# Taking out the matmuls of constants that stand in TensorE's waits in a two-layer hybrid backbone

## Chip, core and metric

The kernel runs on one core of a Trainium2 chip. The metric is the device time of one execution in microseconds, here the median of three timed runs. One more execution was recorded by the hardware profiler; its rows are what the argument uses.

## What is computed

Two layers of a trunk over 512 latent tokens with 256 context tokens ahead of them, model width 1024, all in float32. The reference, cut to the frame of a layer:

```
for l in range(DEPTH):                      # DEPTH = 2
    hx = modulate(rms_norm(x, norm_mix_pre[l]), sh1x, sc1x)
    hc = modulate(rms_norm(h_ctx, norm_mix_pre[l]), sh1c, sc1c)
    y_x, y_c = mixing_layer(hx, hc, ...)    # three head groups, one w_in, one w_out
    x = x + g1x * rms_norm(y_x, norm_mix_post[l])
    hx = modulate(rms_norm(x, norm_mlp_pre[l]), sh2x, sc2x)
    x = x + g2x * rms_norm(sq_relu_mlp(hx, w_mlp1[l], w_mlp2[l]), norm_mlp_post[l])
    if want_ctx: ...                        # the same for h_ctx, layer 1 only
...
def mixing_layer(...):
    zx = split_cols(hx @ w_in_l, IN_SIZES)
    gdn  = gdn_mixer(...)    # gated DeltaNet: triangular solves per chunk, then a scan both ways
    mla  = mla_mixer(...)    # latent attention: softmax(q k^T) v, 4 heads
    hgrn = hgrn_mixer(...)   # HGRN2: gated linear recurrence both ways
    return concatenate([gdn, mla, hgrn]) @ w_out_l
```

The shifts, scales and gates (`sh1x` and so on) come from `silu(c) @ w_ada[l]`.

## The kernel before

All five engines run hand-written queues; an engine waits on counters (semaphores) that others raise. Nothing reorders the work: what stands behind a waiting instruction on its engine waits too. The tokens lie along the columns: a product of 128 rows of outputs has 768 columns (256 of the context, 512 latent), written as two matmuls into a pair of PSUM banks. The second layer leaves out the context where it isn't needed.

The large matrices are multiplied as sums of products of a high and a low part (three matmuls per block of 128 inputs, type float32r, one TensorE instruction each). Plain float32 matmuls take two TensorE instructions each; transposes take one.

The order of a layer on TensorE: the sum of squares of the first norm (`norm0`, in `sum_squares`, lines 900 to 914), the input projection (`gemm_entry`, line 859, which goes through the inputs block by block as POOL and DVE deliver them, then `gemm_parts`), the chunk matrices and triangular inverses of the DeltaNet (lines 1045 to 1148; line 1147 works on blocks which ACT, DVE and POOL have spread out before), its scan, the projection and the levels of the HGRN2 (`level_product`, lines 1294 to 1316: a product of small 32x32 or 64x64 blocks, then DVE and ACT make the factors of the next level from the former ones), `turn_keys` (line 1334, transposes), the sum of squares of its output (`hrms`), attention (`scores`, transposes of the probabilities at line 1457, `output`), the output projection, and the MLP (`mlp_start`, line 1509, and the loop at line 1565). `grms` is the sum of squares of the DeltaNet's output. Columns of `w_ada` for the next modulation (line 970) are worked off in between.

The helper that the change concerns is `hold_clock(dst, n)` (line 832). It issues n matmuls of the constant matrix `ones` with a slice of a constants tile into a piece of PSUM that is free there and is overwritten later with `start=True`; nobody reads the result. It raises no counter. It is called at ten places: at the entry of the input projection (4 in layer 1, 6 in layer 2), ahead of the sums of squares `norm0` (0 and 6), `grms` (3) and `hrms` (1), ahead of line 1045 (1), after the 32x32 inverses (2), in the levels (6 in layer 1), in `turn_keys` (3 and 2), in the first attention steps (4 and 3) and in the MLP's first products (0 and 6). The calls stand between two waits: the first, for the PSUM bank, holds for the filling product too; the second, for the operands, only for the real product behind it. That makes 54 matmuls, 108 TensorE instructions.

## Time and profile before

| | us |
|---|---|
| three timed runs, median | 2350.25 |
| lowest and highest of them | 2344.41, 2350.57 |
| profiled execution | 2344.16 |
| its span, first to last instruction | 2342.3 |
| TensorE busy in it | 2236.3 |
| VectorE, ScalarE, GpSimd busy | 1172.5, 860.8, 222.6 |

The profile names engines by their short names: PE is TensorE's matmuls, PEld its weight loads (which overlap), DVE VectorE, ACT ScalarE, POOL GpSimd, SP the queue that issues DMAs. Times in rows are microseconds from the span's start, unless "ns" is said. PEclk is the granted TensorE clock, 1.00 for 2.4 GHz and 0.50 for 1.2 GHz. The end of a matmul is modelled, and matmuls overlap, so the time that one costs is read from the starts of neighbours. "x12" says that a row merges twelve instructions.

### The profile page before, as it was taken

To read this page: it belongs to the slowest core of one execution; us is meant where nothing else is said; L and a number is where in the kernel's file an instruction comes from. 1 tells how busy PE (TensorE), PEld (TensorE's weight loads), DVE (VectorE), ACT (ScalarE), POOL (GpSimd) and SP (SyncE) were. 2 spreads that over 40 slices of the span, in tenths; PEclk is the share of its full clock that TensorE was granted. 3 is DMA by queue.
4 is the path that set the end of the run, shared out by engine and by line. 5 is a ranking of instruction groups with operands and counts; after the bars stand their busy time and mean duration, and the time that the engine had idled before them with its cause. 6 is when DMAs were issued, how large, how long until landed. Compare 5 with 4: busy or idle time off the path is not lost.

```text
span 2342.3 us, 43142 instructions
## 1 busy us (share of the span) xinstructions
PE 2236.3 (95%) x19310; PEld 1818.3 (78%) x19310; DVE 1172.5 (50%) x1848; ACT 860.8 (37%) x1250; POOL 222.6 (10%) x218
## 2 busy tenths in 40 slices
PE   8999899989999999999999999889997999999998
PEld 5876598876668788888888677659785669888887
DVE  4674353188363651424233587536248456444444
ACT  5362134225464421212123546232324456222233
POOL 3013410000030100000000011421000021000000
PEclk9999999999999999999999999999999999999999
DMA  9217101134301121212121221411116301323222
GB/s 320 64 63 269 53 17 55 55 110 141 104 16 37 37 90 55 72 55 72 54 72 55 91 80 37 150 53 36 55 55 213 120 19 55 108 91 107 90 90 72
DMA packets 161694, 198.42 MB, mean 85 GB/s; under 512 B 18358, under 2 KB 129432, under 8 KB 160871
## 3 DMA queue, kind: packets, MB, share of 16 engines
q1 hardware_dynamic: 155536, 185.20, 24.4%
q10 hardware_dynamic: 5271, 10.10, 1.3%
q8 instruction: 152, 2.49, 0.4%
q0 software_dynamic: 704, 0.37, 0.2%
q14 instruction: 31, 0.25, 0.0%
HBM read 184.60 MB, written 11.06 MB: 84 GB/s over the span
## 4 chain that ended last, share of the span: by engine, by line
PE 86%; DVE 6%; ACT 4%; issue 3%; DMA 0%; POOL 0%; DVEq 0%; ACTq 0%
PE ps L1565 35%; PE ps L857 15%; PE ps L1483 5%; PE ps L1098 3%; PE ps L911 2%; PE ps L1522 2%; PE ps L1418 2%; PE ps L970 2%; PE ps L1237 1%; PE ps L844 1%; PE ps L835 1%; DVE region L2533 1%; PE ps L873 1%; PE ps L1431 1%; PE ps L1457 1%
## 5 line engine op out<-in xcount | busy, mean ns | idle before, releaser
L1565 PE MATMUL ps<-region_r 128*128 128x512 f32 (+1 forms) x1536 | 376.7, 354 | 0.0
L1565 PEld LDWEIGHTS ps<-region_r 128*128 128x128 f32 x1536 | 270.3, 188 | 40.7
L1565 PE MATMUL ps<-region_r,weights_r 128*128 128x512 f32 (+1 forms) x768 | 229.6, 353 | 0.0
L2184 DVE TENSOR_TENSOR weights_r<-weights,region_r 128x2048 fp32r<-128x2048 f32 x62 | 141.9, 2289 | 119.9 <-ACT region_r L1701 119.9
L1565 PE MATMUL ps<-mixed_r,weights_r 128*128 128x512 f32 (+1 forms) x672 | 200.9, 354 | 0.0
L1565 PE MATMUL ps<-modulated_r,region_r 128*128 128x256 f32 (+1 forms) x624 | 186.7, 354 | 0.0
L1565 PE MATMUL ps<-mixed_r,region_r 128*128 128x256 f32 (+1 forms) x624 | 186.6, 353 | 0.0
L2112 ACT ACTIVATE region<-ps,cst 128x768 f32<-128x768 f32 (+1 forms) x64 | 50.2, 795 | 300.8 <-PE ps L1565 281.3
L1565 PEld LDWEIGHTS ps<-region_r,weights_r 128*128 128x128 f32 x768 | 144.3, 188 | 20.5
L2692 DVE TENSOR_TENSOR region_r<-region 128x768 fp32r<-128x768 f32 (+1 forms) x64 | 52.8, 824 | 203.0 <-ACT region L2112 203.0
L1565 PEld LDWEIGHTS ps<-mixed_r,weights_r 128*128 128x128 f32 x672 | 126.3, 188 | 18.0
L1565 PEld LDWEIGHTS ps<-mixed_r,region_r 128*128 128x128 f32 x624 | 117.3, 188 | 16.6
L1565 PEld LDWEIGHTS ps<-modulated_r,region_r 128*128 128x128 f32 x624 | 117.3, 188 | 16.6
L1701 ACT ACTIVATE region_r<-weights 128x2048 fp32r<-128x2048 f32 x62 | 118.5, 1910 | 12.8 <-DMA weights<-in_w_mlp 12.8
L857 PE MATMUL ps<-residual_r,weights_r 128*128 128x512 f32 (+1 forms) x432 | 117.4, 344 | 0.0
L2118 ACT ACTIVATE region<-ps 128x768 f32<-128x768 f32 (+1 forms) x48 | 33.8, 705 | 218.2 <-PE ps L1565 218.2
L2699 DVE TENSOR_TENSOR region<-region 128x768 f32<-128x768 f32 (+1 forms) x32 | 26.4, 825 | 138.9 <-ACT region L2118 138.9
L857 PEld LDWEIGHTS ps<-residual_r,weights_r 128*128 128x128 f32 x432 | 81.1, 188 | 10.6 <-issue 0.2
L857 PE MATMUL ps<-region_r,weights_r 128*128 128x256 f32 x320 | 81.7, 337 | 0.0
L725 POOL CAST region_r<-modulated 128x768 fp32r<-128x768 f32 x16 | 22.7, 1461 | 576.6 <-ACT modulated L1743 576.6
L1098 PE MATMUL ps<-modulated,weights 128*128 128x512 f32 x128 | 69.1, 637 | 5.2 <-issue 4.4
L2191 DVE TENSOR_TENSOR weights_r<-weights,state_r 128x2048 fp32r<-128x2048 f32 x14 | 32.1, 2292 | 82.2 <-ACT state_r L1687 82.2
(435 smaller groups left out, 4809.5 us busy)
## 6 DMA issues: line engine op xcount, KB each, us to landing
weights<-in_w_mlp SPq DMA_DIRECT2D x64, 1024.0 KB, 5.6
weights<-in_w_ada SPq DMA_DIRECT2D x40, 1024.0 KB, 6.1
weights<-in_w_in SPq DMA_DIRECT2D x34, 1024.0 KB, 5.4
region<-in_w_ada SPq DMA_DIRECT2D x8, 1024.0 KB, 16.9
weights<-in_w_out SPq DMA_DIRECT2D x8, 1024.0 KB, 6.7
x_kept<-residual SPq DMA_DIRECT2D x2, 3072.0 KB, 12.4
region<-decays_kept ACTq DMA_DIRECT2D x4, 1536.0 KB, 10.6
residual<-x_kept SPq DMA_DIRECT2D x2, 3072.0 KB, 10.5
```

Of the source, the lines that this page charges most:

```text
L857: last = mm(dst[:, CTX + a:CTX + b], w[:, k, m], r[k][:, a:b], start=(k == 0 and w is high and r is r_high), stop=(k == KB - 1 and r is r_ ...
L911: last = mm(dst[:, CTX + a:CTX + b], mat, sq[:, a:b], start=(k == 0), stop=(k == n - 1))
L970: last = mm(ps[32 * k:32 * k + 32, bank, :], cs[:, 4 * half + k, :], w[:, k, :], start=(half == 0), stop=(half == 1))
L1098: last = mm(ps[:, 6, :], w, Hm[:, k, CTX:TOK], start=(k == 0), stop=(k == KB - 1))
L1418: last = mm(dst[:, CTX + s0:CTX + s1], QH[0:96, h, 128 * qt:128 * qt + 128], KH[0:96, h, s0:s1], start=True, stop=True)
L1483: last = mm(dst[:, at:at + b - a], w[:, k, m], r[:, a:b], start=(k == 0 and part_of == "low"), stop=(k == 5 and w is low))
L1522: last = mm(o, w[:, k, m], r[:, k, a:b], start=(k == 0 and r is Hm_r), stop=(k == KB - 1 and w is low))
L1565: last = mm(dst[:, CTX + a:CTX + b], w[:, k, m], r[:, a:b], start=(k == 0 and r is r_low), stop=(k == KB - 1 and w is low))
L1701: af(mlp_high(j), ring[:, n % NSLOT, :], ACT.Copy).then_inc(w_high_ready, 1)
L2112: copied(l, what, u, af(hid[:, b, lo:], src, ACT.Relu, bias=zero_col))
L2184: v.tensor_tensor(ring_r[:, at, :], ring[:, at, :], mlp_high(j), ALU.subtract).then_inc(w_low_ready, 1)
L2692: v.tensor_tensor(hid_high[:, b, lo:], z, z, ALU.mult)
```

## The change

The helper and all its calls go, with the tables that hold their counts. The waits that stood around a call stay, one behind the other. No other engine's code changes, and no other matmul moves against another.

```diff
-            def hold_clock(dst, n):
-
-                for _ in range(n):
-                    mm(dst, ones, kf[:, 4:8, :].rearrange("p a b -> p (a b)")[:, 0:dst.shape[1]], start=True, stop=True)
...
                 dst = [free_pair(l, "qkv", u) for u in units]
-                hold_clock(dst[0][:, 512:1024], 4 + 2 * l)
...
-                if n0 == 0:
-                    hold_clock(dst[:, 512:1024], {"norm0": 6 * l, "grms": 3, "hrms": 1}.get(what, 0))
...
                 pe.wait_ge(gemm_evac, number(UNITS, l, "qkv", 11) - 2)
-                hold_clock(pair(number(UNITS, l, "qkv", 11) + 1)[:, 512:1024], 1)
                 pe.wait_ge(gs_ready, l + 1)
...
                         pe.wait_ge(u_ready, 2 * NS * (l + 1))
-                        hold_clock(ps[:, 0, :], 2)
                         pe.wait_ge(spread, 12 * (l + 1))
...
-                LEVEL_HOLDS, HOLDS_FROM = ((1, 1, 1), (0, 0)), (5, 2)
...
-                    if lv >= HOLDS_FROM[l]:
-                        hold_clock(ps[:, bank, :], LEVEL_HOLDS[l][j])
                     pe.wait_ge(m_ready, item(l, lv, j))
...
-                    if k < 2:
-                        hold_clock(ps[:, k, :], ((1, 2), (2, 0))[l][k])
...
-                FIRST_HOLDS = ((1, 1, 1, 1), (1, 1, 1, 0))
...
-                    hold_clock(dst[:, 512:1024], FIRST_HOLDS[l][i] if i < 4 else 0)
                     pe.wait_ge(p_ready, a + 1)
...
-                    if p == 1:
-                        hold_clock(dst[0], 6 * l)
```

On TensorE, in the last two levels of layer 1, the queue before reads as follows (`region` holds the factors, `weights,silu_c` are columns of `w_ada`):

```order
2103 L970 MATMUL ps<-weights,silu_c 32x512 x4
2104 L835 MATMUL ps<-k_f_sb 128x512
2105 L1309 MATMUL ps<-region 32x32 x32
2106 L835 MATMUL ps<-k_f_sb 128x512
2107 L1309 MATMUL ps<-region 32x32 x32
2108 L970 MATMUL ps<-weights,silu_c 32x512 x4
2109 L835 MATMUL ps<-k_f_sb 128x512
2110 L1309 MATMUL ps<-region 32x32 x32
2111 L977 MATMUL ps<-row_select,state 128x2 x4
2112 L970 MATMUL ps<-weights,silu_c 32x512 x4
2113 L835 MATMUL ps<-k_f_sb 128x512
2114 L1313 MATMUL ps<-region 64x64 x16
```

and with the change (its lines are numbered anew):

```order
2099 L962 MATMUL ps<-weights,silu_c 32x512 x4
2100 L1296 MATMUL ps<-region 32x32 x64
2101 L962 MATMUL ps<-weights,silu_c 32x512 x4
2102 L1296 MATMUL ps<-region 32x32 x32
2103 L969 MATMUL ps<-row_select,state 128x2 x4
2104 L962 MATMUL ps<-weights,silu_c 32x512 x4
2105 L1300 MATMUL ps<-region 64x64 x32
```

The filling products are gone, and the small products stand directly behind those of `w_ada` or behind each other.

## Rows read from the trace of the kernel before

In a timeline a row gives start, length, engine, line, operation, what is written and read, and in brackets the engine's idle time ahead of it with what ended it. A row of stretches gives the stretch, its length, the busy time (and the instructions) of PE, PEld, DVE, ACT and POOL, then PEclk, the share of the DMA engines and GB/s. A row of waits gives total, times, longest.

**Rows 1.** The page: engines' busy time, chain that ended last.

```profile
span 2342.3 us, 43142 instructions
...
PE 2236.3 (95%) x19310; PEld 1818.3 (78%) x19310; DVE 1172.5 (50%) x1848; ACT 860.8 (37%) x1250; POOL 222.6 (10%) x218
...
PE 86%; DVE 6%; ACT 4%; issue 3%; DMA 0%; POOL 0%; DVEq 0%; ACTq 0%
```

**Rows 2.** All products of line 835, one line's view (durations in ns).

```profile
L835 PE MATMUL ps<-k_f_sb x108: 379/592/697, 42.5 to 1985.5; 128*128 128x512 f32 x96, 128*128 128x256 f32 x12
```

**Rows 3.** Timeline 40 to 50 us: start, us, engine line op, [idle before].

```profile
42.52 3.68 PE L835 MATMUL ps<-k_f_sb 128*128 128x512 f32 x8
...
46.41 0.58 PE L873 MATMUL ps<-region_r,state_r 128*128 128x256 f32 x2 [0.22 <-POOL region_r L725]
```

**Rows 4.** Timeline 1320 to 1372 us.

```profile
1325.24 5.31 PE L835 MATMUL ps<-k_f_sb 128*128 128x512 f32 x12
...
1333.49 12.28 PE L911 MATMUL ps<-mixed,k_f_sb 128*128 128x256 f32 x32 [2.94 <-ACT mixed L1774]
...
1346.86 5.39 PE L835 MATMUL ps<-k_f_sb 128*128 128x512 f32 x12 [1.08 <-ACT region L1656]
...
1350.13 0.96 POOL L725 CAST region_r<-modulated 128x768 fp32r<-128x768 f32 x1 [541.84 <-ACT modulated L1743]
...
1351.68 0.80 PE L873 MATMUL ps<-region_r,state_r 128*128 128x512 f32 x1
```

**Rows 5.** Timeline 289 to 293 us.

```profile
289.46 2.00 ACT L1905 ACTIVATE residual<-ps 32x384 f32<-32x384 f32 x4 [0.40 <-PE ps L1135]
...
290.48 1.98 PE L835 MATMUL ps<-k_f_sb 128*128 128x512 f32 x4 [1.22 <-DVE mixed L2417]
...
292.39 0.27 PE L1147 MATMUL ps<-mixed,region 64*64 64x64 f32 x1
```

**Rows 6.** Timeline 585.6 to 588.5 us.

```profile
586.25 1.58 ACT L1628 ACTIVATE region<-mixed 128x768 f32<-128x768 f32 x2 [7.74 <-DVE mixed L2593]
...
586.76 1.13 PE L835 MATMUL ps<-k_f_sb 128*128 128x512 f32 x2 [1.02 <-DVE cst L2600]
```

**Rows 7.** Timeline 640 to 652 us, first attention steps.

```profile
640.37 1.12 PE L835 MATMUL ps<-k_f_sb 128*128 128x512 f32 x2 [0.59 <-ACT region L2040]
...
644.30 1.91 ACT L1693 ACTIVATE region_r<-weights 128x2048 fp32r<-128x2048 f32 x1
```

**Rows 8.** Busy time in stretches, with the granted clock.

```profile
220.50:227.10 6.60, 3.39 (x63) 2.00 (x66) 0.56 (x1) 0.00 (x0) 1.26 (x1) 1.00 0.37 137
...
522.50:529.33 6.83, 6.23 (x173) 4.49 (x176) 5.29 (x12) 1.94 (x4) 0.00 (x0) 0.50 0.61 197
...
1334.88:1338.29 3.41, 3.41 (x7) 2.02 (x6) 3.41 (x5) 1.71 (x3) 0.00 (x0) 0.50 0.00 0
1491.90:1495.30 3.40, 0.00 (x0) 0.00 (x0) 3.32 (x10) 0.00 (x0) 0.00 (x0) 1.00 0.00 0
1495.30:1498.70 3.40, 2.82 (x4) 1.17 (x4) 0.43 (x4) 2.04 (x3) 0.00 (x0) 0.50 0.55 198
798.98:802.39 3.41, 3.41 (x10) 2.63 (x9) 3.41 (x6) 1.68 (x3) 1.38 (x2) 0.50 0.00 0
802.39:805.80 3.41, 3.41 (x17) 2.81 (x16) 3.41 (x5) 1.77 (x3) 1.38 (x2) 1.00 0.00 0
541.70:565.70 24.00, 21.95 (x371) 11.84 (x367) 20.58 (x49) 18.45 (x41) 0.00 (x0) 1.00 0.60 200
```

**Rows 9.** Timeline 1794 to 1806 us, end of the levels.

```profile
1797.97 1.98 PE L835 MATMUL ps<-k_f_sb 128*128 128x512 f32 x4
...
1801.67 0.66 PE L1347 MATMUL ps<-k_f_sb,region 128*128 128x128 f32 x4 [0.41 <-ACT mixed L2009]
```

**Rows 10.** The core's span and mean granted clock.

```profile
core 0: 2342.3 us, clock 0.990
```

**Rows 11.** Who waited for whom, PE, longest in total.

```profile
PE ps L1309 <- issue: 13.2, 8, 3.4
```

## Prediction

> **What bounds the kernel now.** I read the page first: TensorE is busy 95% of the span and the chain of work that ended last is 86% TensorE [rows 1]. So almost all of the time is matmuls that stand in one queue, and a product that nobody reads costs its length unless the engine would have waited there anyway. The view of line 835 comes next: 108 instructions (54 products of constants, two instructions each), from 42.5 us to 1985.5 us [rows 2]. They stand in 28 groups. Twelve of them take 5.3 us, 0.44 us each [rows 4], so all of them hold the engine for some 47 us, 2% of the span. The question is how much of that was a wait in any case. For that I went through the timeline at each of the 28 groups and compared the start of the next real product with the moment at which the thing it waits for was done. Last I read the granted clock in short stretches [rows 8], because without these products the engine stands idle for longer, and in this trace its clock stands at the lower of its two levels (1.2 instead of 2.4 GHz) in some short stretches.
>
> **What the removal gives back, kind by kind.**
> (a) *Groups inside a wait.* At 42.52 us eight instructions end before the next product starts at 46.41, which POOL releases, with 0.22 us of idle time still in front of it [rows 3]. The twelve at 1325.24 end 2.94 us before the product at 1333.49, which waits for an ACT square [rows 4]. Four more groups look like this (two of 2 instructions ahead of line 1045, two of 6 ahead of the sum of squares of `grms`, with 0.4 to 0.9 us still idle), and so does the group of 12 short ones at the last layer's MLP, behind which the next product starts as DVE delivers. That is 48 of the 108 instructions, and they give back nothing: the releaser is another engine that does not wait for them. What covers them is the normalisation chain on ACT, DVE and POOL.
> (b) *The diagonal blocks' copy.* The four instructions at 290.48 run until the next product at 292.39, while the last of ACT's four copies ends at 289.46 + 2.00 = 291.46 [rows 5]. Without them the product starts some 0.9 us earlier; the same place in the second layer gives 1.0. Together 1.9 us.
> (c) *The sum of squares of `hrms`.* The product behind the two instructions at 586.76 needs the first of two ACT squares, done at about 586.25 + 0.8 = 587.1, and starts when they are through, at 587.7 [rows 6]. That is 0.6 us, in both layers 1.2 us.
> (d) *The entry of layer 2.* The twelve at 1346.86 are followed by the product at 1351.68 with no idle time, but the first POOL cast it reads is only ready at 1350.13 + 0.96 = 1351.09 [rows 4]. So 5 us of filling hide a real wait of almost the same length, and 0.5 us comes back.
> (e) *The levels of layer 1.* Eighteen instructions stand between 541.7 and 563.9 us, about 9 us of TensorE's time, all without idle time around them. But this is a ping-pong with DVE, which is busy 20.58 of 24.00 us there [rows 8]. The gain cannot be over DVE's idle 3.4 us. It may be nothing, if the next DVE step is late for another reason. I take 1.2 us, a third of the slack, since ACT too is at 18.45 of 24.00 and is waited for at the end of the stretch. In layer 2 the four at 1797.97 take 1.8 us, but the product at 1801.67 waits for ACT [rows 9], which is in one piece of work since before them: nothing.
> (f) *The first attention steps.* Seven groups of two, 0.9 us each, 6.5 us in sum, again without idle time behind them (the first is at 640.37 [rows 7]). In layer 1 ACT has a weight conversion of 1.91 us from 644.30 on in its queue [rows 7], and the evacuation of the transposes stands behind it, so what the first steps gain is waited for again. Between 0.5 and 6.5 us; I take 3.0 us (1.2 in layer 1, 1.8 in layer 2), nearer the lower end for that reason.
> Sum of the gains: 1.9 + 1.2 + 0.5 + 1.2 + 3.0 = **7.8 us**, with ends at 4 us (1.9 + 1.2 + 0.5 + 0 + 0.5) and 15 us (3.6 + 3.4 + 1.8 + 6.5).
>
> **What the clock takes.** The mean granted clock is 0.990 [rows 10]: 2342 x 0.010 = 23 us lost, so 47 us at half, some 7 of them at the very end, where nothing dense runs. That is about eleven low stretches of 3.41 us now. The price of one low stretch: from 798.98 to 802.39 the clock is at half and 10 products start, in the equally long stretch after it 17 [rows 8]. Seven of 17 lost in 3.41 us is 1.4 us, and half of 3.41 us, 1.7 us, is the most. I take 1.5 us where dense products follow.
> How often? Before, the engine is idle 3.40 us and more ahead of 1495.3 and the clock is low from there on; it is low from 522.50 to 529.33 behind an idle time of 3.4 us (the longest of line 1309 [rows 11]), and from 1334.88 on behind the 2.94 us at 1333.49 [rows 4, 8]. From 220.5 on TensorE stands still for 3.2 of 6.6 us, waiting for its instructions, and the clock stays up [rows 8]. So of four idle times of 2.9 us and more three were followed by a low stretch. After the removal there are: 42.65 to 46.4 (3.7 us) [rows 3] and three like it of 3.0 to 3.4 us (the two ahead of `grms` and the last MLP): 4 x 0.75 = 3.0 low stretches. 1345.77 to 1351.1 (5.3 us) [rows 4]: 1. The 8.1 us ahead of 1333.49 already had one; what follows there waits for an ACT square every 1.7 us, so a longer low stretch costs about a third of one. Four of 1.8 to 2.3 us (ahead of line 1045 and at the place of (b)), a size behind which the clock mostly stayed up: 1.3. The levels and the attention steps, where 9 and 6.5 us of dense products go out between small ones: 1.5. In sum 7.1 low stretches, x 1.5 us = **10.7 us**. Bounds: 2 stretches (3 us) and 14 (21 us).
>
> **Sum.** -7.8 + 10.7 = +2.9 us. The profiled execution took 2344.2 us (span 2342.3), so it would be 2347.1 with the change; it is at the lower edge of the three timed runs, whose median, 2350.25, lies 6.1 us higher, and I add the difference to that median: **2353 us**. A measurement of this kernel can tell about 0.3%, 7 us, from no change, and the forecast lies inside that.
>
> **Rivals.**
> *Slower, by the clock everywhere.* Place: the first dense products behind each wait that was filled. If every one of the 6 long idle times is followed by a low stretch, the 4 middle ones too, and the levels and attention steps of both layers add 4, that is 14 x 1.5 = 21 us against 7.8: +13 us, 2363 us. It decides from (7.05 + 7.8) / 1.5, about 10 low stretches more than now. For it: three of four; the weak filling that is left between waits in the levels; and a low stretch slows the products that others wait for. Against it: 220.5 us, and that a part of a low stretch falls into the idle time itself and costs nothing.
> The Trainium skill, page "TensorE: Matmul & The Clock Gate", section "HAM oscillation — how this bites in real kernels", says that TensorE's clock is halved after a longer wait and that each burst then starts slow, every time. That rule speaks against this change and would make it this rival; the trace agrees in three of the four long idle times and not in the one at 220.5 us.
> *Faster, the clock hardly reacts.* If only one or two new low stretches appear, mostly inside idle time, cost 0 to 2 us, the gains of 7.8 us remain or are somewhat larger: 2343 us or less. Against it: the idle times of 3.7, 5.3 and 8.1 us.
> *The gains do not arrive.* TensorE waits 13.2 us at line 1309 with the releaser "issue" [rows 11], that is, for nothing that the profile shows but its own instructions. If filling products gave that supply time to catch up, the gain of (e) and part of (f) turn into such waits: gains 5 us, +6 us, 2356 us. This stays within 0.3% alone and is in the forecast's chance.
>
> **Chances.** Forecast (within 0.3%, with the third rival in it) 0.52, slower 0.38, faster 0.10. The range reaches from the edge of the faster rival, 2343, to a little above the slower one's value, 2365, since one time in ten may lie beyond either end.
>
> **What would show it.** In the trace after: no line 835, TensorE busy for some 45 to 50 us less by the page's count apart from slower products; idle times of about 3.7 us ahead of the first product of the entry, 8 and 5.3 us around 1325 to 1351, and the waits of (a) with the same releasers. For the gains: the product behind ACT's copies at 291.5, the one of `hrms` 0.6 us earlier. For the price: 15 to 21 low stretches in place of eleven, with half as many products in those that follow the entries of both layers. The prediction is wrong if the number of low stretches grows by over 10 or by less than 2, or if one of them lasts for several times 3.4 us, or if the levels shrink by far over 3.4 us.

## The result and the profile after

The change makes the kernel slower: 2366.29 us against 2347.78 us for the kernel before on the same chip (medians of six runs each), a ratio of 1.0087 with a 95% interval of 1.0073 to 1.0101, that is about 20 us (18.5 us by the medians). The forecast was 2353 us, a step of 2.9 us up (a ratio of 1.0012) that could not be told from no change, with a range up to 2365 us. What came is clear of no change, and the time lies outside the range.

Some words are used throughout. A *filling product* is one of the 54 that `hold_clock` issues. A *low period* is an unbroken time at half clock, and a *stretch* is 3.41 us of it, the shortest that these traces show. A *place* is a part of the kernel, found again in each trace by its products. "Waits without a releaser" are those which the profile marks "issue".

In this section and the next the lines are those of the changed kernel, numbered anew: 867 for 873 (first products of the input projection), 903 for 911 (sums of squares), 1089 for 1098 (the gate's products between the inverses), 1113, 1123 and 1138 for 1122, 1132 and 1148 (inverses), 1296 and 1300 for 1309 and 1313 (levels). First its page, and its clock, to be held against [rows 1, 10]:

```profile
span 2364.7 us, 42940 instructions
...
PE 2221.9 (94%) x19202; PEld 1820.8 (77%) x19202; DVE 1173.0 (50%) x1848; ACT 861.3 (36%) x1250; POOL 222.4 (9%) x218
...
PE 86%; ACT 5%; DVE 4%; issue 3%; DMA 1%; POOL 0%; DVEq 0%; ACTq 0%
```

```profile
core 0: 2364.7 us, clock 0.973
```

TensorE has 108 instructions less and is busy 14.4 us less, not the 45 to 50 us that the filling products held, while the span is 22.4 us longer than 2342.3. The clock fell from 0.990 to 0.973: 0.027 x 2364.7 = 64 us lost against 23 us, so 128 us at half in place of 47. Read period by period, the clock was low in 25 periods, against 11 before. Without the last one of each, in the tail, where nothing dense runs, they come to 117 us against 35.5 us: 24 low stretches of 3.41 us more. Nine of the 24 periods ahead of the tail are longer than one stretch (6.8 or 10.2 us).

Some of the periods, as busy time in windows of the trace (columns as in [rows 8]; the last four columns are POOL's busy time, the clock, the DMA engines' share and GB/s). After:

```profile
45.00:51.85 6.85, 5.09 (x16) 4.44 (x17) 6.06 (x5) 6.85 (x12) 6.85 (x6) 0.50 1.01 430
51.85:58.70 6.85, 6.85 (x41) 6.00 (x41) 6.85 (x6) 3.15 (x4) 4.52 (x4) 1.00 0.06 22
573.00:595.30 22.30, 22.30 (x234) 22.23 (x234) 12.87 (x41) 7.26 (x11) 0.00 (x0) 0.85 0.01 1
1580.50:1598.80 18.30, 15.50 (x247) 13.67 (x243) 5.07 (x12) 10.87 (x21) 2.04 (x2) 0.81 0.08 29
1338.70:1348.90 10.20, 4.37 (x7) 2.53 (x8) 10.20 (x13) 8.84 (x8) 0.00 (x0) 0.50 0.00 1
```

The same products before, in the entry of layer 1, the state updates and outputs of the HGRN2 behind `turn_keys` (called the read-out below) and the end of layer 2's inverses:

```profile
46.40:53.20 6.80, 6.79 (x39) 5.98 (x40) 6.80 (x5) 6.80 (x12) 6.80 (x6) 1.00 0.83 354
566.00:585.00 19.00, 19.00 (x234) 18.93 (x233) 12.87 (x41) 7.11 (x11) 0.00 (x0) 1.00 0.01 2
1563.00:1576.40 13.40, 13.40 (x247) 11.92 (x244) 5.07 (x12) 10.89 (x21) 2.04 (x2) 1.00 0.02 6
```

The pairs are the first two rows of after with the first of before, the third with the second, the fourth with the third; the last row of after is the one at `norm0` of layer 2. The read-out gives the price cleanly. The same 234 products, all without idle time, take 19.00 us at full clock and 22.30 us with 6.8 us at half: 3.30 us for two stretches, 1.65 us each. At the end of the inverses 247 products go from 13.40 us to 18.30 us. Of these 4.9 us, 2.8 us are time in which TensorE is not busy (15.50 of 18.30), and 2.1 us are slower products.

Some of the waits of TensorE in the whole run after (total, times, longest):

```profile
PE ps L1296 <- issue: 16.1, 11, 3.1
PE ps L903 <- ACT region L1609: 10.8, 6, 3.5
PE ps L867 <- POOL region_r L725: 9.2, 2, 5.5
PE ps L903 <- ACT mixed L1755: 8.2, 1, 8.2
```

Of the lower three little was to be seen before: at the same line TensorE waited 2.3 us in sum for ACT's squares, 2.9 us at the one of `norm0` [rows 4], and for POOL 0.22 us at the first entry [rows 3]; the rest of the time was filled. The first row answers to [rows 11], with eleven waits for eight.

Holding the start of each product against that of the same product before gives the 22.4 us by place. "Low" is the change in time at half clock.

| place, in us of before | span, us | low, us | predicted here, us |
|---|---|---|---|
| start and entry of layer 1 (to 58) | +2.6 | +6.8 | +1.1 |
| norm and first inverses of layer 1 (169 to 306), gain (b) | +1.9 | +6.8 | -0.9, +1.1 |
| `grms`, layer 1 (390 to 400) | +1.4 | +3.4 | +1.1 |
| scan and projection (400 to 541), no filling there | +3.5 | +3.9 | 0 |
| levels, layer 1 (541 to 566), gain (e) | -2.5 | +2.9 | -1.2 and a share of +2.2 |
| read-out of the HGRN2 (566 to 585) | +3.3 | +6.8 | |
| `hrms` and attention, layer 1 (585 to 652), gains (c), (f) | 0.0 | +6.8 | -1.8 and a share of +2.2 |
| MLP of layer 1 (652 to 1324), no filling there | +0.7 | 0.0 | 0 |
| `norm0`, layer 2 (1324 to 1345) | +0.5 | +6.8 | +0.5 |
| entry of layer 2 (1345 to 1365), gain (d) | +0.7 | +3.5 | +1.0 |
| inverses of layer 2 (1490 to 1577), gain (b) | +10.3 | +20.4 | -1.0, +0.9 |
| `grms` to the levels, layer 2 (1577 to 1804) | -0.5 | +6.9 | +1.1 |
| read-out, `hrms`, attention, layer 2 (1804 to 1982) | -1.1 | +3.4 | -2.4 |
| MLP entry, layer 2 (1982 to 1995) | +1.5 | +3.4 | +1.1 |

Nearly half of the loss stands in one place, the triangular inverses of layer 2, where only two of the 54 products were taken out. A second profile of each kernel shows what of this repeats: after again has +9.7 us there, and the kernel before once has +3.2 us against itself. Over the span the second profiles are 2357.1 us (clock 0.975) and 2345.8 us (0.989).

### The profile page after: what moved, and what is told of

The parts are those of the page before. It is cut to its first block, busy times and chain, and to the rows that moved or that the text cites. A ratio compares the mean times of both kernels' runs of the same rounds, so it can differ in the third digit from the quotient of the medians.

```text
span 2364.7 us, 42940 instructions
## 1 busy us (share of the span) xinstructions
PE 2221.9 (94%) x19202; PEld 1820.8 (77%) x19202; DVE 1173.0 (50%) x1848; ACT 861.3 (36%) x1250; POOL 222.4 (9%) x218
## 4 chain that ended last, share of the span: by engine, by line
PE 86%; ACT 5%; DVE 4%; issue 3%; DMA 1%; POOL 0%; DVEq 0%; ACTq 0%
PE ps L1546 35%; PE ps L852 15%; PE ps L1466 4%; PE ps L1089 3%; PE ps L903 2%; PE ps L962 2%; PE ps L1503 2%; PE ps L1403 2%; PE ps L1227 1%; PE ps L867 1%; PE ps L1245 1%; PE ps L839 1%; PE ps L1416 1%; PE ps L1440 1%; PE ps L1346 1%
## 5 line engine op out<-in xcount | busy, mean ns | idle before, releaser
L852 PEld LDWEIGHTS ps<-residual_r,weights_r 128*128 128x128 f32 x432 | 81.1, 188 | 10.5 <-issue 0.2
## 6 DMA issues: line engine op xcount, KB each, us to landing
region<-decays_kept ACTq DMA_DIRECT2D x4, 1536.0 KB, 10.7
residual<-x_kept SPq DMA_DIRECT2D x2, 3072.0 KB, 10.2
```

Of the source, the lines that this page charges most:

```text
L852: last = mm(dst[:, CTX + a:CTX + b], w[:, k, m], r[k][:, a:b], start=(k == 0 and w is high and r is r_high), stop=(k == KB - 1 and r is r_ ...
```

## Experiments

None of the experiments changes a result that is used, since nobody reads the filling products. Edits are against the kernel before, and "..." marks what is left out between their parts. The time that stands behind "against" is the median of the kernel before, measured together with the experiment. Figures by place are against the first profile of the kernel before.

### Which group of products matters

**e1_long** keeps the 28 products in the long waits (entries, `norm0`, `grms`, MLP) and takes the other 26 out:

```diff
-                    hold_clock(dst[:, 512:1024], {"norm0": 6 * l, "grms": 3, "hrms": 1}.get(what, 0))
+                    hold_clock(dst[:, 512:1024], {"norm0": 6 * l, "grms": 3, "hrms": 0}.get(what, 0))
...
-                hold_clock(pair(number(UNITS, l, "qkv", 11) + 1)[:, 512:1024], 1)
...
-                        hold_clock(ps[:, 0, :], 2)
...
-                LEVEL_HOLDS, HOLDS_FROM = ((1, 1, 1), (0, 0)), (5, 2)
+                LEVEL_HOLDS, HOLDS_FROM = ((0, 0, 0), (0, 0)), (5, 2)
...
-                        hold_clock(ps[:, k, :], ((1, 2), (2, 0))[l][k])
+                        hold_clock(ps[:, k, :], ((0, 0), (0, 0))[l][k])
...
-                FIRST_HOLDS = ((1, 1, 1, 1), (1, 1, 1, 0))
+                FIRST_HOLDS = ((0, 0, 0, 0), (0, 0, 0, 0))
```

> Of the 54 filling products of before, 28 are kept, those in the long waits: entry of the input projection, norm0, grms, the MLP's first products. The rest is out, as in the changed kernel. Local theory (each filling keeps the clock up only for the products right behind its own wait): in the comparison of the two traces the stretches behind these waits cost +2.3 us (to 57.6), +1.4 (390 to 399), +0.7 (1334 to 1365) and +1.5 us (1982 to 1995), and up to 1.7 us between 400 and 500; these 6 to 8 us come back, so 2359 us, with 26 or so low stretches of 3.41 us. Rival (low stretches come by where the run happens to stand against the chip's own time, and move whenever a kernel changes): the low stretches of 1501 to 1577 move or go as well, the sum is anywhere between 2350 and 2366, and the stages named don't answer one by one.

Measured: 2356.62 us against 2346.84, ratio 1.0054 [1.0030, 1.0078], clock 0.983. Entries, `grms`, and the MLP entry are back at 0.0 us; the read-out has +3.3 us as after, the inverses of layer 2 +6.7 us. So the fillings of the long waits account for a part, and more than a half of the loss comes with them in place.

**e2_steps** keeps only the 18 products of the levels, `turn_keys` and attention:

```diff
-                hold_clock(dst[0][:, 512:1024], 4 + 2 * l)
...
-                    hold_clock(dst[:, 512:1024], {"norm0": 6 * l, "grms": 3, "hrms": 1}.get(what, 0))
+                    hold_clock(dst[:, 512:1024], {"norm0": 0, "grms": 0, "hrms": 0}.get(what, 0))
...
-                hold_clock(pair(number(UNITS, l, "qkv", 11) + 1)[:, 512:1024], 1)
...
-                        hold_clock(ps[:, 0, :], 2)
...
-                        hold_clock(dst[0], 6 * l)
+                        pass
```

> Kept are the 18 filling products of the levels, turn_keys and the first attention steps; the 36 others are out. Local theory: the stage from 541 to 652 us, which came out at about +0.8 us in sum with gains of 2.5 and 0.9 us and losses of 3.3 and 1.3 us, goes back to before's; in layer 2 the attention's gain of 1.6 us is given up. About 2366 us, as the changed kernel within 2 us. Rival: as for e1_long, low stretches elsewhere move by chance, 2355 to 2370.

Measured: 2366.37 us, 1.0095 [1.0072, 1.0118], clock 0.971. The total came as expected, by way of two misses that the expectation did not have: the read-out has +4.9 us although its fillings stand as before, and the inverses of layer 2 +7.8 us.

**e3_gdn** keeps only the eight products of the DeltaNet's inverses and `hrms` (in each layer one ahead of line 1045, two ahead of line 1147 and one in `hrms`):

```diff
-                hold_clock(dst[0][:, 512:1024], 4 + 2 * l)
...
-                    hold_clock(dst[:, 512:1024], {"norm0": 6 * l, "grms": 3, "hrms": 1}.get(what, 0))
+                    hold_clock(dst[:, 512:1024], {"norm0": 0, "grms": 0, "hrms": 1}.get(what, 0))
...
-                LEVEL_HOLDS, HOLDS_FROM = ((1, 1, 1), (0, 0)), (5, 2)
+                LEVEL_HOLDS, HOLDS_FROM = ((0, 0, 0), (0, 0)), (5, 2)
...
-                        hold_clock(ps[:, k, :], ((1, 2), (2, 0))[l][k])
+                        hold_clock(ps[:, k, :], ((0, 0), (0, 0))[l][k])
...
-                FIRST_HOLDS = ((1, 1, 1, 1), (1, 1, 1, 0))
+                FIRST_HOLDS = ((0, 0, 0, 0), (0, 0, 0, 0))
...
-                        hold_clock(dst[0], 6 * l)
+                        pass
```

> Kept are the 8 filling products ahead of line 1045, ahead of line 1147 (after the inverses) and ahead of the hrms sum; the 46 others are out. Local theory: the stages 289 to 306 and 1559 to 1577 go from +0.2 and +4.0 us to zero, so some 4 us come back, 2362 us; the +6.5 us between 1490 and 1550, where no filling stood in either kernel, stay. Rival: the stages from 1490 to 1577 change together, since what matters is where the low stretches begin, and 6 to 10 us come back or none.

Measured: 2369.95 us, 1.0111 [1.0092, 1.0129], clock 0.971. Expected was 2362: a clear miss. The end of the inverses, with its two filling products in front as before, is longer by 4.8 us. Its window, to be held against the last row of before above, except that it also takes in three of the four filling instructions:

```profile
1582.60:1600.80 18.20, 16.87 (x250) 13.37 (x250) 5.07 (x12) 10.90 (x22) 2.04 (x2) 0.85 0.04 12
```

The timeline says where the 4.8 us lie: 2.9 us between the first filling instruction and the second, of which 2.75 us are a wait without a releaser that ends at 1583.93, 1.3 us in the three filling instructions behind it, which run at half clock, and only 0.6 us behind the filling.

**e4_no_inv2** takes out only these two products, in layer 2:

```diff
-                        hold_clock(ps[:, 0, :], 2)
+                        hold_clock(ps[:, 0, :], 2 * (1 - l))
```

> The kernel before, without the two filling products ahead of line 1147 in layer 2 alone (4 of 108 instructions). Local theory: the stretch 1563 to 1577 loses 5.0 us and the wait gives back 1.0: +4 us, 2352 us, with one more low stretch of 6.8 us and nothing else changed. Rival (the 5.0 us of the changed kernel came of where the low stretches stood after 18 us of delay, not of the two products): within 1 us of before.

Measured: 2349.43 us, 1.0011 [1.0000, 1.0022]; the end of the inverses +0.8 us, the whole place +1.0 us. The local theory, by which each filled wait keeps the clock up for the stage behind it, expected 4 us here. Its step from the missing filling to a low period is borne out: a stretch is low from 1568.2 us, right behind the place of the two products, and costs 1.8 us against the 0.9 us gained. In all six profiles without the two (this one, both of after, e1, e2, e5) a low period lies there, with them in two of ten (e3, e11). The size is what falls: the 5 us that after loses there are not reached without the others, and keeping the two in e3 does not save the place. In after and in e3 a wait without a releaser of 2.8 us stands there, which e4 does not have.

### The place in the instruction stream

If it is not the filling in front alone, it may be something that shifts with the number of filling products. Each of them is four instructions of TensorE's stream (two weight loads, two matmuls), and the inverses are 32x32 and 64x64 products that go out in bursts, between which TensorE waits for nothing that the profile shows. These waits in the inverses of layer 2, before and after:

```profile
PE ps L1122 <- issue: 5.0, 5, 1.3
PE ps L1098 <- issue: 4.4, 1, 4.4
PE ps L1132 <- issue: 3.0, 5, 1.0
```

```profile
PE ps L1113 <- issue: 6.0, 4, 2.9
PE ps L1089 <- issue: 4.4, 1, 4.4
PE ps L1123 <- issue: 3.7, 4, 1.6
PE ps L1138 <- issue: 2.8, 1, 2.8
```

The 4.4 us at line 1098 (1089 after) are in both, and are a wait for DVE, as e11_placed shows below; they are left out of what is called the waits without a releaser of this stage. The rest is 8.0 us before, 12.5 us after (8.1 and 13.9 us in the second profiles); that of after includes the 2.8 us at line 1138 that ate gain (b) there.

**e5_same_count** puts in the place of each product the same number of instructions, waits on a counter that has long been high enough (two such waits share one instruction):

```diff
-                for _ in range(n):
-                    mm(dst, ones, kf[:, 4:8, :].rearrange("p a b -> p (a b)")[:, 0:dst.shape[1]], start=True, stop=True)
+                for _ in range(8 * n):
+                    pe.wait_ge(const_in, 16)
```

> The changed kernel's matmuls, with every filling product replaced by as many TensorE instructions that only wait for a counter which was reached long ago. So the instruction stream has the length and the places of before, and nothing fills. Stream theory: part of the 19 us is not the clock but TensorE's own instruction supply (waits with the releaser issue grew from 7.5 to 12.2 us between 1500 and 1584), which hangs on where in the stream the bursts of small products stand; then those waits go back to about 7 us there, the stage loses its 9.6 us in large part, and the time is 2354 to 2360. Clock theory alone: the time stays at 2366 within 2 us, and the issue waits of that stage, too, stay at 10 us or more, since they grew by slower matmuls or by chance.

Measured: 2362.45 us against 2345.93, ratio 1.0061 [1.0043, 1.0080], clock 0.974. The inverses of layer 2 are back at +1.0 us, with 6.6 us of such waits, though the fillings are as absent as after. In the whole run, too, the waits without a releaser are back: 37.3 us before, 45.3 us after, 37.0 us here. Those of the inverses:

```profile
PE ps L1098 <- issue: 4.4, 1, 4.4
PE ps L1122 <- issue: 3.4, 4, 1.6
PE ps L1132 <- issue: 3.2, 3, 1.5
```

Most of the slowdown stays, since the clock stays down; the read-out now has +6.2 us and that of layer 2 +4.9 us. So most of the +10.3 us of the inverses goes with the place in the stream, and most of the rest of the loss does not: it comes with the missing fillings alone, by the clock.

**e6_shift** does the opposite: all 54 products stay, and 112 instructions of the same kind are put into the input projection of layer 2, where the queue is full of dense work:

```diff
+                            for _ in range(14 if (l, what, load) == (1, "qkv", 3) else 0):
+                                pe.wait_ge(const_in, 16)
```

> The kernel before with all its filling products, and 112 instructions that only wait for a counter reached long ago put between the dense products of layer 2's input projection (loads 3). They shift the instruction stream of layer 2 against 256 so that its inverse stage stands as in the changed kernel. Stream theory: the stretch from 1490 to 1577 costs 3 to 8 us more with larger issue waits, about 2353 us. Clock theory alone: within 2 us of before.

Measured: 2354.49 us against 2345.93, ratio 1.0032 [1.0018, 1.0047], clock 0.985; its layer 2 inverses begin 1.6 us later than before, and they themselves have +8.8 us. Their waits:

```profile
PE ps L1124 <- issue: 8.7, 5, 3.3
PE ps L1100 <- issue: 4.8, 2, 4.4
PE ps L1134 <- issue: 2.9, 3, 1.3
PE ps L1149 <- issue: 2.0, 1, 2.0
```

Line 1124 is 1122 before. The waits without releaser are 14.0 us, 6.0 us more than before, and two more low stretches can make up the rest. Work that is the same to the last product costs some 8 us more (7.5 us by the ratio, 8.6 us by the medians) because what stands in front of it has shifted.

**e9_shift64** and **e10_shift192** are the same with 8 and 24 in place of 14, that is 64 and 192 instructions.

> The kernel before with 64 more waiting instructions in layer 2's input projection (e6_shift had 112), so its inverse stage stands at 203 against 256 in TensorE's instruction stream; before stands at 139, the changed kernel at 255. Stream theory: the issue waits between 1490 and 1580 are again not those of before (7.4 us) and the time moves with them by up to 8 us, most likely up. Rival: shifts other than 112 do nothing, within 1.5 us of before.

> The same with 192 more, which puts the inverse stage of layer 2 at 75 against 256, where it stood in e1_long (73). Stream theory: as in e1_long the stretch from 1490 to 1577 costs 5 to 7 us more than in before, with issue waits of about 10 us; 2352 us. Rival: what e1_long showed there came of its missing filling product ahead of line 1045 or 1147, and the time is that of before within 1.5 us.

Measured: 2350.37 us and 2352.22 us against 2346.66, ratios 1.0014 [1.0003, 1.0024] and 1.0025 [1.0012, 1.0037]. The inverses: +5.5 and +4.6 us, waits without a releaser 10.5 and 8.9 us. In e10 the 192 waits themselves also cost 2.7 us where they stand; they are not free in such numbers. All kernels but e11_placed side by side, with the place of the stage's products in TensorE's instruction stream modulo 256 (the remainder when the instructions in front of them are divided by 256):

| kernel | place | waits without releaser, us | the inverses of layer 2, us |
|---|---|---|---|
| before, second profile | 139 | 8.0, 8.1 | 0, +3.2 |
| e4_no_inv2 | 139 | 6.9 | +1.0 |
| e12_levels_out, e8_entry_out | 139 | 8.5, 9.2 | +2.0, +2.7 |
| e7_att_out | 144 | 9.6 | +2.7 |
| e5_same_count | 147 | 6.6 | +1.0 |
| e9_shift64 | 203 | 10.5 | +5.5 |
| e6_shift | 251 | 14.0 | +8.8 |
| after, second profile | 255 | 12.5, 13.9 | +10.3, +9.7 |
| e3_gdn | 17 | 13.4 | +12.1 |
| e2_steps | 47 | 13.4 | +7.8 |
| e1_long | 73 | 10.7 | +6.7 |
| e10_shift192 | 75 | 8.9 | +4.6 |

The modulus was my choice at first; the values go up to one side of the circle and come down again. The traces hold more than the waits, though: the DMA queue that brings the instructions. In the page of the kernel before it reads (packets, MB, share of the engines):

```profile
q8 instruction: 152, 2.49, 0.4%
```

That is 16 KB a packet and, with TensorE's 2 x 19310 records, some 64 bytes an instruction, so that a packet holds about 256 of TensorE's instructions: the modulus. And each wait ends behind a packet. The one of 2.8 us at line 1138 after ends at 1583.60 us, and a packet runs from 1581.4 to 1582.3; the one of 2.75 us between the filling instructions of e3 ends at 1583.93, with a packet from 1581.6 to 1582.6. In the sixteen profiles the inverses of layer 2 have 142 waits without a releaser, and every one ends 1.2 to 1.6 us behind the end of such a packet, while only 13% of the stage's time lies 1.1 to 1.7 us behind one. So these are waits for TensorE's instructions, and where a burst of small products stands against the packets decides how long they are. What decides when a packet is sent for is not shown.

### The parts one by one

The next three take a part out and leave as many instructions in its place, so that nothing behind it shifts. The edit calls `same_count`, which holds the loop of e5_same_count, in place of `hold_clock` at the places named. The fourth, e11_placed, is a placement of its own and does not keep the count.

**e7_att_out** (attention and `hrms`, nine products):

> The kernel before, with the 9 filling products of the first attention steps and of the hrms sums replaced by as many instructions that only wait for a counter reached long ago. In every profile without them the stages behind them were shorter at an unchanged clock (2.3 us from 1865 to 1982, 0.4 us twice at hrms, 0.6 to 0.9 us at 641). Gain theory: 3.5 to 4.5 us faster than before, about 2342 us, with no more low stretches. Rival: the clock takes it back somewhere behind (as once at 652), no difference within 1.5 us.

Measured: 2344.38 us (twelve runs) against 2346.66, ratio 0.9993 [0.9979, 1.0007]. The places themselves give -0.4, -0.9, -0.4, -1.6 and -0.8 us, 4.1 us in all and as expected, with no low stretch there. Elsewhere one low stretch stands in the levels of layer 1 (from 551.8 us, +1.6 us), the inverses of layer 2 have +2.7 us and its `norm0` -1.5 us, so that the profile ends where that of before does. The time cannot be told from no change, where 3.5 to 4.5 us were expected.

**e8_entry_out** (entries of both layers, ten products):

> The kernel before, with the 10 filling products at the entries of both layers' input projection replaced by as many instructions that only wait for a counter reached long ago. Clock theory: +1.5 to 2.8 us up to 57.6 and +1.2 less 0.4 us around 1352 to 1365, the rest unchanged: +3 us, 2349 us. Rival (the low stretches there came of delays upstream): within 1 us of before.

Measured: 2354.11 us against 2346.66, ratio 1.0026 [1.0014, 1.0038]: 6 to 7.5 us where 3 were expected. The profile has the expected places (+1.5, -0.4, +1.5 us), but it is of the lowest of ten runs (2346.71), so it does not show where the others lose more. That they lose it to the clock is on record: it is 0.986 and 0.987 in the two lowest runs and 0.980 to 0.984 in the other eight.

**e12_levels_out** (levels and `turn_keys`, eleven products):

```diff
-                        hold_clock(ps[:, bank, :], LEVEL_HOLDS[l][j])
+                        same_count(LEVEL_HOLDS[l][j])
...
-                        hold_clock(ps[:, k, :], ((1, 2), (2, 0))[l][k])
+                        same_count(((1, 2), (2, 0))[l][k])
```

> The kernel before, with the 11 filling products of the levels and turn_keys replaced by as many instructions that only wait for a counter reached long ago; all other fillings stay. Clock theory: as in every profile without them, the stretch 541 to 566 gains 1.5 to 2.8 us and the stretch 566 to 585 loses 3.3 to 6.3 us with 7 to 13 us of low clock; in layer 2 (1797 to 1819) up to +4.9 us; together +3 to +6 us, 2351 us. Rival (these low stretches come with those of the other missing fillings, since delays upstream move them): within 1.5 us of before.

Measured: 2353.69 us against 2345.92, ratio 1.0034 [1.0018, 1.0051], clock 0.983, some 8 us where 3 to 6 were expected. The levels give back 0.5 us, and the read-out behind them, with no idle time in it, costs 6.2 us. Its window in this kernel, and in the second profile of the kernel before, whose code is unchanged there:

```profile
568.60:593.80 25.20, 25.20 (x233) 25.13 (x233) 12.88 (x41) 7.19 (x10) 0.00 (x0) 0.74 0.01 1
```

```profile
565.90:586.55 20.65, 20.65 (x234) 20.58 (x234) 12.87 (x41) 7.23 (x11) 0.00 (x0) 0.92 0.01 2
```

Four low stretches in a row, 13.7 us, in the one; in the other one stretch, and 1.65 us, without any change of the kernel. These products have 64 and 128 columns, and a low period that begins among them can go on through several stretches. Taking the fillings of the levels out brings it on: the read-out costs 3.3 to 6.3 us more in all six profiles without them (after, its second profile, e1, e3, e5, e12), and 0 or 1.6 us more in nine of the ten with them. Having them does not exclude it (+4.9 us in e2).

**e11_placed** tries a better placement: no fillings in attention, `hrms` and ahead of line 1045, more in `norm0` (9) and in the MLP of layer 1 (4), and three new ones in the 4.4 us wait at line 1098 of layer 2:

```diff
+                if l:
+                    pe.wait_ge(ada_read, 2 * l + 1)
+                    hold_clock(ps[:, 6, :], 3)
```

> A version made of the findings: no filling products in the attention, at hrms and ahead of line 1045 (gains, no low stretch seen behind them); 3 more at norm0 of layer 2 (9 for 6), 3 new ones at layer 2 ahead of the gate products (idle 4.4 us in before, a low stretch behind it each time), 4 at layer 1's MLP entry (idle 1.9 us, a low stretch at 799 now and then). Layer 2's inverse stage stands at 156 against 256 in the stream (before 139). Clock theory: -4 us by the attention and hrms, -1.2 at 1335 to 1345, -1 at 1495, -0.5 at 799: 2341 us, 0.25% faster. Rival: the stream's place costs it again 2 us or more, and new low stretches come elsewhere: 2344 to 2347.

Measured: 2348.55 us (twelve runs) against 2345.92, ratio 1.0014 [1.0004, 1.0025]; expected was a gain of 5 us. Its timeline from 1495 to 1506 us:

```profile
1495.51 0.95 PE L977 MATMUL ps<-row_select,region 128*128 128x2 f32 x8
...
1500.60 0.15 DVE L2396 COPY cst<-modulation 128x1 f32<-128x1 f32 x1
...
1500.81 5.49 PE L835 MATMUL ps<-k_f_sb 128*128 128x512 f32 x6 [4.35 <-DVE cst L2396]
...
1506.10 1.26 PE L1097 MATMUL ps<-modulated,weights 128*128 128x512 f32 x2
```

The 4.4 us, without a releaser in before, are a wait for a DVE copy, which the kernel before also has just ahead of the product:

```profile
1495.62 0.15 DVE L2396 COPY cst<-modulation 128x1 f32<-128x1 f32 x1
...
1495.88 2.04 PE L1098 MATMUL ps<-modulated,weights 128*128 128x512 f32 x2 [4.39 <-issue]
```

The edit puts the wait for the counter that this copy raises ahead of the new products, so they stand behind the wait and not in it, and the gate's first product starts 5.3 us after the wait has ended: +4.0 us in this place. The other places gave about what was hoped (-1.5 us at `norm0`, -2.8 us in attention and `hrms` of layer 2), and the clock took back some: at 1469 us, where the product ahead of line 1045 was missing, a low stretch came (+1.6 us), at 652 us another (+1.4 us).

By their ratios the isolated parts are 6 us (entries), 8 us (levels and `turn_keys`), 7.5 us (shift, at about the worst place) and -1.6 us (attention, not to be told from nothing). What the products of `grms`, `norm0`, the MLP and line 1045 do alone was not measured. No kernel tried is measurably faster than the one before.

## Why the prediction missed

**The bound and the covers** were right: TensorE is as much the chain after as before (86%), and the products of (a) were inside waits. In the kernel after, the same releasers end the waits. At the entry of layer 1 (start, length, engine line, [idle before]):

```profile
44.87 11.50 POOL L725 CAST region_r<-modulated 128x768 fp32r<-128x768 f32 x8 [34.89 <-ACT modulated L1724]
...
46.76 0.98 PE L867 MATMUL ps<-region_r,state_r 128*128 128x256 f32 x2 [3.74 <-POOL region_r L725]
...
48.18 0.84 PE L867 MATMUL ps<-region_r,state_r 128*128 128x256 f32 x2
...
52.64 0.52 PE L867 MATMUL ps<-region_r,state_r 128*128 128x256 f32 x2
```

The product waits for the POOL cast, as in [rows 3], and gained nothing. And around layer 2's first norm and entry:

```profile
1344.53 12.73 PE L903 MATMUL ps<-mixed,k_f_sb 128*128 128x256 f32 x32 [8.18 <-ACT mixed L1755]
...
1361.62 0.96 POOL L725 CAST region_r<-modulated 128x768 fp32r<-128x768 f32 x1 [542.41 <-ACT modulated L1724]
...
1362.72 0.77 PE L867 MATMUL ps<-region_r,state_r 128*128 128x512 f32 x1 [5.46 <-POOL region_r L725]
...
1363.29 0.63 PE L867 MATMUL ps<-region_r,weights_r 128*128 128x512 f32 x1
```

8.18 us and 5.46 us are idle where 8.1 and 5.3 were expected, and the first product of the entry starts 0.14 us behind the end of the first cast (1361.62 + 0.96).

**The gains** were mostly right. (b) gave 0.8 + 1.0 us for 1.9, but in layer 2 a wait of 2.8 us without a releaser stood in front of the next product after, which the step had no term for. (c) gave 0.42 + 0.43 us for 1.2; the product of after starts a little behind the end of the first square (timeline of after, layer 1):

```profile
596.56 1.58 ACT L1609 ACTIVATE region<-mixed 128x768 f32<-128x768 f32 x2 [7.73 <-DVE mixed L2574]
...
597.55 2.82 PE L903 MATMUL ps<-region,k_f_sb 128*128 128x256 f32 x8 [1.49 <-ACT region L1609]
```

By the same reading as in the prediction the square is done at about 596.56 + 0.8 = 597.36, and the product starts at 597.55, 0.2 us later. (d) gave 0.44 for 0.5 us. (e) gave 2.5 us in layer 1 with 2.9 us more at low clock in it, and 0.5 us in layer 2, for 1.2 us; the bound of 3.4 us held. (f) gave 0.9 + 2.4 = 3.3 us for 3.0. The sum, 9.3 us, stands against 7.8 us, and the range of 4 to 15 us held.

**The price of a low stretch** was about right where dense products follow: 1.5 us predicted, 1.65 us measured.

**How often** is the step that failed: the term of 7.1 low stretches more, with a bound of 14, measured 24. It failed in three ways.
*It counted an idle time as at most one stretch.* Of the 24 periods ahead of the tail, nine last two or three. At the entry of layer 1, 6.8 us are low (16 instructions where the next 6.85 us have 41), and in the timeline pairs of products start 0.64 us apart until 51.4 us and 0.35 us apart from 52.3 us on. The low stretch at 1334.88 that already was there [rows 8] became 10.2 us. There the judgment that it costs little held: the product stream waits for ACT and `norm0` lost 0.5 us. Ahead of `grms` an idle time of 3.52 us brought one, for 1.4 us, as reckoned:

```profile
398.02 3.03 ACT L1609 ACTIVATE region<-mixed 128x768 f32<-128x768 f32 x4
...
399.00 7.09 PE L903 MATMUL ps<-region,k_f_sb 128*128 128x256 f32 x16 [3.52 <-ACT region L1609]
```

In layer 2 a wait of 3.09 us at the same place brought none in this kernel, and one in e2, e3 and e5. The wait at 220.5 us, which the prediction set against a fall, does not speak so clearly: in the second profile of the kernel before, a wait of 3.13 us at this place ends at 222.3, and the clock is low from 223.7 to 227.1.
*It gave the levels, `turn_keys` and attention 1.5 stretches together.* In the levels and the read-out of layer 1 alone they are 9.7 us, three, and 20.5 us, six, in e12. What was not seen is that the loss does not fall where the filling stood: the levels get shorter, and the read-out behind them, which has no idle time, is low and pays in full. The prediction had a row that could have warned of it, the period of 6.83 us at 522.50 [rows 8], amid small products.
*It had no term for places without a filling.* From 400 to 541 us +3.5 us, and in layer 2's inverses ahead of 1563 us +6.3 us, come without any filling product missing there.

**The place in the stream** was seen as the third rival, with the right rows (waits with the releaser "issue" [rows 11]) and the wrong form. It was priced at 3 us of gains that would not arrive, for filling that gives the supply time. What e6 shows is that the waits of layer 2's inverses grow by 6 us with all fillings in place, when 112 instructions are put in front. In after this is 4.5 us in layer 2's inverses and 5.4 us in the levels (13.2 us at line 1309, 16.1 + 2.5 us at 1296 and 1300), of which the levels' may be in part DVE's time anyway, busy 20.58 of 24.00 us there [rows 8]. How much of the 20 us it makes in all is known only roughly: by the ratios of after and e5, 1.0087 - 1.0061, some 6 us, by their medians against before, 18.5 and 16.5 us, some 2 us, and the intervals overlap.

**The sum again, with what was measured:** -9.3 us of gains, some 6 us of waits by the place in the stream (an estimate: 4.5 us in layer 2's inverses, 1.1 us around a wait of 1.96 us that ends at 503.0 us at full clock), and 24 stretches for what is then left of the +22.4 us of span in this profile, 26 us or 1.1 us each. That is less than 1.65 us, and many do lie partly in idle time or beside a wait for another engine. Of the rivals, "slower, by the clock everywhere" had the right mechanism and the larger part of the size (+13 us), with ten stretches too few; with its chance of 0.38 it stood behind the forecast. The Trainium skill, page "TensorE: Matmul & The Clock Gate", section "HAM oscillation — how this bites in real kernels", which the prediction weighed against one stretch at 220.5 us, has each burst behind a longer wait start slow: at the entries, the first `grms` and the last MLP of this trace that is so, at layer 2's `grms`, behind 3.09 us, the shortest of these waits, it is not.

What stays open: why a low period lasts one stretch in one execution and four in another (the kernel before itself ranges from 2339.7 to 2353.1 us over 35 runs), whether waits for instructions themselves bring low stretches on (in after 20.4 us more are low in the inverses, in e6 6.8 us with as long waits), and at which places e8 loses its other 3 to 4 us.

## What to carry over

A product that nobody reads, in a wait that is there anyway, can be worth its place: 54 of them held TensorE for 47 us and gave back only 9 us when they went, and without them, by the sum above, some 26 us were lost to the clock. Count what an idle time does to the clock in stretches and not in times: nine of 24 low periods here lasted two or three. Look for the loss also in the next stage that has no idle time, and not only where the filling stood. Before an edit of TensorE's queue is judged by a place where many small products go out, put the same number of instructions back: a shift alone moved this kernel by 0.3%.

## What was not expected of the hardware

The low periods ahead of the tail last 3.4, 6.8, 10.2 or 13.7 us in all sixteen profiles, the longest (e12_levels_out, from 567.9 us) in a stage that is busy without a gap.

Bursts of 32x32 and 64x64 products wait for their own instructions, up to 4.4 us at a time (e2_steps, ending at 1582.9 us), and the sum of these waits in the same stage runs from 6.6 us to 14.0 us with the number of instructions issued far ahead of it. All 142 of them in that stage end 1.2 to 1.6 us behind a 16 KB packet of the instruction queue.

A wait shown without a releaser can be one for another engine: the 4.4 us at line 1098 are DVE's, which the profile named only when another instruction stood first behind the wait.

Waits that are satisfied are nearly free among dense products: 112 instructions of them in the input projection of layer 2 cost too little to be seen there, but 192 cost 2.7 us.
